# A two-layer block on one core: decay chain moved behind the gated products, one sigmoid moved ahead of two copies, and three transposes moved inside matmul units

## The reference

```python
u_lat = _modulate(h_lat, sh_m, sc_m)
q, k, v, g, glu, gates = _split_proj(u_lat @ p['w_in'] + p['b_in'])
lg_f = log_sigmoid(p['ret_decay_fwd']); lg_b = log_sigmoid(p['ret_decay_bwd'])   # 8 heads each
s_f = _retention_final_state(k_c, v_c, lg_f)          # context keys weighted by exp(distance * lg)
o, _, _ = _retention_bidir(q, k, v, lg_f, lg_b, s_f, s_b)
ret = silu(g) * _head_norm(o)
y_a = ret @ p['w_ret_out']
za, zb = split(glu); z = za * sigmoid(zb)             # the gated product
z = silu(_layernorm(_depthwise_conv(z, 31 taps)))
y_b = z @ p['w_conv_out'] + p['b_conv_out']
ga, gb = split(sigmoid(gates))
mix = (ga * y_a + gb * y_b) @ p['w_mix_out'] + p['b_mix_out']
```

## Time and profile before

| | |
|---|---|
| median of 3 runs | 1573.7 us |
| profiled execution | 1574.86 us, span 1573.0 us |
| TensorE busy | 1489.7 us, 95% of the span |
| VectorE, ScalarE, GpSimd busy | 708.4, 577.0, 411.3 us |
| mean granted TensorE clock | 0.988 of full speed |
| the stretch that the change touches | about 57 to 130 us, and 399 to 515 us |

### The profile page before, as it was taken

The page is one execution under the profiler, slowest core; times in us unless marked ns, Lnnn a source line. Parts: engine busy times, 40 slices in busy tenths (PEclk is TensorE's granted clock), DMA queues, the critical chain, the costliest instruction groups (busy, mean ns, idle before and its releaser), DMA issues.

```text
span 1573.0 us, 22932 instructions
## 1 busy us (share of the span) xinstructions
PE 1489.7 (95%) x9454; PEld 1033.6 (66%) x9454; DVE 708.4 (45%) x1292; ACT 577.0 (37%) x781; POOL 411.3 (26%) x314
## 2 busy tenths in 40 slices
PE   5999999999999899999999999889999899999998
PEld 3788888888666644444344344368888678878786
DVE  2578887575544841121111111244422644343674
ACT  2442425454343312222122112334344355465553
POOL 0000000010000100000000000149887686757564
PEclk9999999999999899999999999989999999999999
DMA  9722224436688789999999999747556353444432
GB/s 321 243 89 99 81 81 154 134 107 218 240 303 311 290 349 426 427 428 428 429 427 429 428 429 427 310 139 230 171 181 210 122 180 112 134 134 134 134 107 94
DMA packets 107330, 381.18 MB, mean 242 GB/s; under 512 B 7782, under 2 KB 9614, under 8 KB 94958
## 3 DMA queue, kind: packets, MB, share of 16 engines
q1 hardware_dynamic: 107246, 380.02, 63.9%
HBM read 378.95 MB, written 1.05 MB: 242 GB/s over the span
## 4 chain that ended last, share of the span: by engine, by line
PE 70%; DMA 15%; DVE 4%; ACT 4%; issue 1%; POOL 1%; SPq 0%; ACTq 0%; DVEq 0%; POOLq 0%
DMA arena<-in_w_exp_up 14%; PE ps L797 12%; PE ps L798 12%; PE ps L806 11%; PE ps L1222 9%; PE ps L1232 3%; PE ps L990 3%; PE ps L989 3%; PE ps L996 3%; PE ps L880 2%; ACT w_hi L2538 1%; PE ps L1243 1%; PE ps L1389 1%; POOL w_lo L2457 1%; DMA ring<-in_w_ret_out 1%
## 5 line engine op out<-in xcount | busy, mean ns | idle before, releaser
L2457 POOL TENSOR_TENSOR w_lo<-ring,w_hi 128x512 fp32r<-128x512 f32 x280 | 375.1, 1380 | 128.0 <-ACT w_hi L2538 116.3
L2538 ACT ACTIVATE w_hi<-ring 128x2048 fp32r<-128x2048 f32 x130 | 246.5, 1911 | 294.6 <-PE ps L806 130.8
L797 PE MATMUL ps<-w_hi,xt_hi 128*128 128x512 f32 x512 | 202.0, 394 | 0.0
L798 PE MATMUL ps<-w_hi,xt_lo 128*128 128x512 f32 x480 | 187.0, 390 | 0.0
L1526 DVE TENSOR_TENSOR w_lo<-ring,w_hi 128x2048 fp32r<-128x2048 f32 x60 | 138.0, 2303 | 93.1 <-ACT w_hi L2538 92.8
L1222 PE MATMUL ps<-arena 128*32 128x512 f32 x1408 | 155.4, 593 | 10.0 <-DMA arena<-in_w_exp_up 9.0
L797 PE MATMUL ps<-w_hi,yt_hi 128*128 128x512 f32 x352 | 139.6, 397 | 5.5 <-ACT w_hi L2538 3.0
L2457 POOL TENSOR_TENSOR w_lo<-ring,w_hi_ahead 128x512 fp32r<-128x512 f32 x8 | 9.9, 1275 | 480.3 <-ACT w_hi_ahead L2862 477.6
L806 PE MATMUL ps<-w_lo,xt_hi 128*128 128x512 f32 x512 | 126.7, 390 | 1.8 <-POOL w_lo L2457 1.8
L1222 PEld LDWEIGHTS ps<-arena 128*32 128x32 f32 x1408 | 49.7, 110 | 113.4 <-issue 112.1
L2120 DVE TENSOR_SCALAR selT<-ps 128x256 fp32r<-128x256 f32 x32 | 13.6, 424 | 237.8 <-ACT arena L2874 237.8
(11 more groups left out here) (328 smaller groups left out, 2361.3 us busy)
## 6 DMA issues: line engine op xcount, KB each, us to landing
arena<-in_w_exp_gate SPq DMA_DIRECT2D x22, 2048.0 KB, 29.9
arena<-in_w_exp_up SPq DMA_DIRECT2D x22, 2048.0 KB, 34.3
arena<-in_w_exp_down SPq DMA_DIRECT2D x21, 2048.0 KB, 33.5
ring<-in_w_in SPq DMA_DIRECT2D x40, 1024.0 KB, 5.1
ring<-in_b_w_in SPq DMA_DIRECT2D x40, 1024.0 KB, 5.1
ring<-in_a_w_in SPq DMA_DIRECT2D x24, 1024.0 KB, 5.1
ring<-in_w_exp_down SPq DMA_DIRECT2D x11, 2048.0 KB, 32.5
ring<-in_w_exp_gate SPq DMA_DIRECT2D x10, 2048.0 KB, 29.9
```

The costliest lines, as they stand in the source:

```text
L797: pe.matmul(o[:, tt, :], hi[:, k, x_], w[:, c, :], start=(bias is None and j == 0 and c == 0), stop=False)
L798: pe.matmul(o[:, tt, :], lo[:, k, x_], w[:, c, :], start=False, stop=False)
L2457: ins = pool.tensor_tensor(w_lo2[:, slots_of[n], k, :], ring[:, slots_of[n], k, :], w[:, k, :].bitcast(F32), ALU.subtract)
L2538: act.activation(part_of(n)[1][:, :, :], ring[:, slots_of[n]], ACT.Copy).then_inc(S("w_hi_full"), 1)
```

## The change

Five edits, all in the order of the lists; two of them also move work between places of one list:

1. VectorE: everything that computes the decays goes from ahead of `modulate(1, 0)` to later places. The two small operations stand behind `lo_of("glu", 3, 1)`, the chain and its four products behind `lo_of("k", 0, 1)`. `lo_of("glu", 2, 1)` now follows `lo_of("glu", 1, 1)` directly. Behind the chain come 12 taps in place of 20, then the scale of `wdec` with its wait for ScalarE's second Exp, then `lo_of("k", 1, 0)`. The 8 taps are left to later calls of `conv_taps`, which ends at the same total.
2. ScalarE: the first Exp goes behind `sigmoid_z(1)`, the second behind `turned_z(1)`.
3. ScalarE: `sigmoid_gate(3)` goes ahead of `lead_ret(2)` and `lead_ret(3)`.
4. TensorE: `turn_conv(0)` goes inside `ret_unit(1, 3)`, `turn_conv(1)` inside `conv_unit(0, 0)`, `turn_merged(1)` inside `mix_unit(0, 0)`, each as its `between`. The waits for the transposed halves move into `conv_unit`.
5. ScalarE and VectorE follow: `spread(3)` between the two conv halves, `gate_ret(1)` between their rests, `merge(1)` ahead of `lo_of("mix", 0, 0)`, `lead("mix", 1, 0)` ahead of `lead_part("mT", 1, ...)`.

```diff
@@ TensorE
+            def conv_unit(t, j, between=None):
+                if t == 0:
+                    pair_evacuated(pe, ("cvT", j))
+                gemm_unit("conv", t, j, xt2_hi, cv_lo, bias=BIAS_ROWS["conv"] + t, between=between)
             def turn_conv(c):
+                pe.wait_ge(S("cz_ready"), 1)
...
-            ret_unit(1, 3)
+            ret_unit(1, 3, between=lambda: turn_conv(0))
             spread_tail(3)
-            pe.wait_ge(S("cz_ready"), 1)
-            turn_conv(0)
-            turn_conv(1)
-            pair_evacuated(pe, ("cvT", 0))
-            conv_unit(0, 0)
+            conv_unit(0, 0, between=lambda: turn_conv(1))
             tail_unit(4, 0)
-            pair_evacuated(pe, ("cvT", 1))
...
-            mix_unit(0, 0)
-            turn_merged(1)
+            mix_unit(0, 0, between=lambda: turn_merged(1))
@@ VectorE (the moved chain and definitions are unchanged)
             lo_of("glu", 1, 1)
+            lo_of("glu", 2, 1)
+            modulate(1, 0)
+            u_rest(1, 0)
+            gated(0)
+            lo_of("glu", 3, 0)
+            modulate(1, 1)
+            u_rest(1, 1)
+            lo_of("glu", 3, 1)
             dve.wait_ge(S("load_decays"), 48)
...
-            lo_of("glu", 2, 1)
+            conv_taps(6)
+            lo_of("k", 0, 0)
+            gated(1)
+            lo_of("k", 0, 1)
             dve.wait_ge(S("decay_exped"), 1)
...
+            conv_taps(12)
             dve.wait_ge(S("decay_exped"), 2)
             dve.tensor_scalar(wdec, wdec, DK ** -0.5, None, ALU.mult).then_inc(S("wdec_ready"), 1)
-            conv_taps(20)
             lo_of("k", 1, 0)
...
-            for c in range(2):
-                rest_part("cvT", c, xt2_hi, cv_lo)
+            rest_part("cvT", 0, xt2_hi, cv_lo)
             gate_ret(1)
+            rest_part("cvT", 1, xt2_hi, cv_lo)
...
+            merge(1)
             lo_of("mix", 0, 0)
-            merge(1)
@@ ScalarE
             lead("glu", 2, 1)
-            (wait decay_asked 1, Exp of la)
             sigmoid_z(0)
...
             turned_z(0)
-            (wait decay_asked 2, Exp of wdec)
...
             sigmoid_z(1)
+            (wait decay_asked 1, Exp of la)
...
             turned_z(1)
+            (wait decay_asked 2, Exp of wdec)
...
             lead("ret", 0, 0)
+            sigmoid_gate(3)
             lead_ret(2)
             lead_ret(3)
-            sigmoid_gate(3)
...
             lead("conv", 0, 0)
+            lead_part("cvT", 0, xt2_hi)
             spread(3)
-            for c in range(2):
-                lead_part("cvT", c, xt2_hi)
+            lead_part("cvT", 1, xt2_hi)
...
             product_rows("tail", 5, 9)
+            lead("mix", 1, 0)
             lead_part("mT", 1, ot_hi)
             spread(5)
-            lead("mix", 1, 0)
```

More of the change, by code:

```diff
@@ L1087, in _, with ret_unit, mix_unit @@
             turn_ret(3)
-            def ret_unit(t, j):
+            def ret_unit(t, j, between=None):
                 if t == 0:
                     pair_evacuated(pe, ("retT", j))
[L1092 to L1097, removed]
+                gemm_unit("ret", t, j, yt_hi, rt_lo, nk=4, at=KC, between=between)
+            def conv_unit(t, j, between=None):
+                if t == 0:
+                    pair_evacuated(pe, ("cvT", j))
+                gemm_unit("conv", t, j, xt2_hi, cv_lo, bias=BIAS_ROWS["conv"] + t, between=between)
+            def mix_unit(t, j, between=None):
                 pair_evacuated(pe, ("mT", j))
-                gemm_unit("mix", t, j, ot_hi, ot_lo, bias=BIAS_ROWS["mix"] + t)
+                gemm_unit("mix", t, j, ot_hi, ot_lo, bias=BIAS_ROWS["mix"] + t, between=between)
             def tail_unit(t, j):
@@ L1591, in _ @@
             lo_of("glu", 1, 1)
[L1592 to L1595, removed]
             lo_of("glu", 2, 1)
[L1597 to L1626, removed]
             modulate(1, 0)
@@ L1683, in _ @@
             lo_of("glu", 3, 1)
-            dve.wait_ge(S("decay_exped"), 2)
-            dve.tensor_scalar(wdec, wdec, DK ** -0.5, None, ALU.mult).then_inc(S("wdec_ready"), 1)
+            dve.wait_ge(S("load_decays"), 48)
+            link(dve.tensor_scalar(la[:, 0, :], lg, -1.0, None, ALU.mult))
+            settle()
+            dve.tensor_tensor(la[:, 0, :], la[:, 0, :], lg, ALU.min).then_inc(S("decay_asked"), 1)
             conv_taps(6)
@@ L1689, in _ @@
             lo_of("k", 0, 1)
-            conv_taps(20)
+            dve.wait_ge(S("decay_exped"), 1)
+            link(dve.tensor_scalar(la[:, 1, :], la[:, 0, :], 2.0, None, ALU.add))
+            settle()
+            link(dve.reciprocal(la[:, 1, :], la[:, 1, :]))
+            settle()
+            link(dve.tensor_tensor(la[:, 0, :], la[:, 0, :], la[:, 1, :], ALU.mult))
+            settle()
+            link(dve.tensor_tensor(la[:, 1, :], la[:, 0, :], la[:, 0, :], ALU.mult))
+            settle()
+            link(dve.tensor_scalar(la[:, 2, :], la[:, 1, :], 2.0 / 17, 2.0 / 15, ALU.mult, ALU.add))
+            settle()
+            for n in (13, 11, 9, 7, 5, 3, 1):
+                link(dve.tensor_tensor(la[:, 2, :], la[:, 2, :], la[:, 1, :], ALU.mult))
+                settle()
+                link(dve.tensor_scalar(la[:, 2, :], la[:, 2, :], 2.0 / n, None, ALU.add))
+                settle()
+            link(dve.tensor_tensor(la[:, 2, :], la[:, 2, :], la[:, 0, :], ALU.mult))
+            link(dve.tensor_scalar(lg, lg, 0.0, None, ALU.min))
+            settle()
+            link(dve.tensor_tensor(lg, lg, la[:, 2, :], ALU.subtract))
+            settle()
+            dve.wait_ge(S("load_decays"), 48)
+            for d in range(2):
+                for tt in range(NT):
+                    ins = dve.tensor_scalar(wdec[:, d, tt, :], lg[:, H * d:H * (d + 1)], pos[:, d, tt:tt + 1], None, ALU.mult)
+                    if d == 1 and tt == 1:
+                        ins.then_inc(S("decay_asked"), 1)
+                    else:
+                        link(ins)
+            conv_taps(12)
+            dve.wait_ge(S("decay_exped"), 2)
+            dve.tensor_scalar(wdec, wdec, DK ** -0.5, None, ALU.mult).then_inc(S("wdec_ready"), 1)
             lo_of("k", 1, 0)
@@ L2634, in _ @@
             lead("glu", 2, 1)
-            act.wait_ge(S("decay_asked"), 1)
-            act.activation(la[:, 0, :], la[:, 0, :], ACT.Exp).then_inc(S("decay_exped"), 1)
             sigmoid_z(0)
@@ L2641, in _ @@
             turned_z(0)
-            act.wait_ge(S("decay_asked"), 2)
-            act.activation(wdec, wdec, ACT.Exp).then_inc(S("decay_exped"), 1)
             evacuate_x(3)
@@ L2649, in _ @@
             sigmoid_z(1)
+            act.wait_ge(S("decay_asked"), 1)
+            act.activation(la[:, 0, :], la[:, 0, :], ACT.Exp).then_inc(S("decay_exped"), 1)
             lead("k", 1, 0)
@@ L2653, in _ @@
             turned_z(1)
+            act.wait_ge(S("decay_asked"), 2)
+            act.activation(wdec, wdec, ACT.Exp).then_inc(S("decay_exped"), 1)
             lead("v", 0, 0)
```

## The result

The changed kernel takes 1563.1 us (median of six runs, 1558.1 to 1571.6) against 1572.9 us (median of six, 1570.7 to 1574.6). The ratio is 0.9946 with a 95% interval of 0.9928 to 0.9964. In a second series it was 1563.0 us, ratio 0.9949 (0.9921 to 0.9978). The profiled execution took 1563.49 us, its span 1561.6 us: 11.4 us under the profiled execution of before. The medians differ by 9.8 and 9.7 us. The intervals of the ratios (5.7 to 11.3 us and 3.5 to 12.4 us) hardly tell these from the 11.5 us of the forecast; what is missing was found in the profiles, term by term.

The account below looks back on a forecast made before the run. The prediction took TensorE, busy for 95% of the span, as the bound, leaving only its stops and half clock to regain. Terms 2.4 + 3.8 + 1.5 + 3.6 + 0.2 = 11.5 us gave 1562.2 us from 1573.7, range 1560.2 to 1567.0.

Parts of the forecast that it names:

- Part A, the stop: Ahead of `turn_z(0)`: stop shrinks from 2.70 to 0.67 us; with half clock and glu (3, 1)'s 0.48 us, 3.9 us gained.
- Part A, the new wait: At k (1, 0): TensorE waits 1.5 us for VectorE's remainder behind the second Exp; bounds nothing to 3.1 us.
- Part A, what else is queued: VectorE's later remainders lag 7 to 8 us at v (0, 0), with 4.8 us of cover left; counted as nothing.
- Part B: Ahead of ret (0, 0): sigmoid before the copies removes the stop, 2.2 us, and half clock, 1.6 us; 3.8 us.
- Part C: Ahead of conv (0, 0): moving the conv transposes removes the 1.5 us wait and none replaces it; 1.5 us.
- Part D: Ahead of mix (1, 0): an earlier leading part removes the stop, 2.0 us, and half clock, 1.6 us; 3.6 us.
- The half clock: Behind the stops of 2.70, 2.16 and 2.02 us TensorE runs at 1.2 GHz; 1.4, 1.6 and 1.6 us regained.
- Transposes as a pause: Rival, 4%: the 0.67 us stop plus 16 transposes count as one pause, 1.4 us is not regained; 1563.6 us.
- A new fall of the clock: Rival, 17%: half clock follows the 1.5 us stop at k (1, 0) or a like one; 1563.8 to 1565.4 us.
- Unit loads taking it back: Rival, 9%: full DMA engines set the pace, so the ret (0, 0) gain and half of mix's are lost; 1567.9 us.
- VectorE as the bound: Rival, 4%: from k (1, 0) on, ten remainders up to q (0, 1) each come 1.5 us late; 1577.2 us.
- The edit not doing what it says: Rival, 4%: another semaphore holds ret (0, 0) and mix (1, 0), so their stops stay; 1569.6 us.

Follow-up runs that it names:

- before_again: The kernel before the change, no edit, profiled a second time: 1572.6 us, span 1570.8 us.
- only_a: The kernel before with only VectorE's and ScalarE's order around the decays changed: 1569.4 us, ratio 0.9977 (ten runs).
- only_b: The kernel before with only `sigmoid_gate(3)` moved ahead of `lead_ret(2)` and `lead_ret(3)`: 1567.7 us, ratio 0.9964 (ten runs).
- only_c: The kernel before with only the conv transposes moved inside ret (1, 3) and conv (0, 0), copies and rests split accordingly: 1569.6 us, ratio 0.9987 (ten runs).
- only_d: The kernel before with only the mix edits (transposes, merge, leading part of mix (1, 0)): 1570.0 us, ratio 0.9983 (ten runs).
- fill_b: The kernel before with 20 unused identity transposes where TensorE stood still 2.16 us ahead of ret (0, 0): 1569.9 us (one run).
- after_again: The changed kernel once more, no edit, beside the kernel before: 1563.0 us (12 runs), ratio 0.9949.

## Why the prediction came out right, and where it didn't

The median was forecast at 1562.2 us and measured at 1563.1; the profiled execution at 1563.4 and measured at 1563.49. The near hit of the second is partly luck in how terms compensate:

- **Part A, the stop.** Forecast 2.70 to 0.67 us, measured 0.70 (0.70 in every profile that has the change). The 0.48 us stop went. Right. Its size of 0.48, though, belongs to the half clock ahead of it, as the point on the half clock shows.
- **Part A, the new wait.** Forecast 1.5 us, measured 1.35 to 1.39 in four profiles, released by w_lo, VectorE idle for 10.6 us ahead. Right. Its bound above, half clock behind it, never came.
- **Part A, what else is queued.** A step that failed: "all of VectorE's later remainders" was worked out for v (0, 0) and found covered, which holds, but the rope also frees a bank pair, and TensorE's context tile of k 1 needs that. 0.46 us more. The list of who waits for a delayed engine has to hold its releases of buffers, and not only its products. A gave 1.92 us for 2.4.
- **Part B.** Forecast 3.8 us, measured 3.67 up to ret (0, 3), where the stop grew from 0.98 to 1.28 us.
- **Part C.** Forecast 1.5 us, 1.8 in the changed kernel and 0.8 alone. The wait went, as forecast; how much of it is kept hangs on when conv (0, 0)'s and ret (1, 3)'s units land, and alone the part kept nothing up to the first expert.
- **Part D.** Forecast 3.6 us, measured 4.3 up to the first expert. The forecast cause holds in every part: the unit had landed, and only ScalarE's order kept it. The 0.2 us added for pipeline fills can't be told apart at these landmarks.
- **The half clock.** The term that was mis-sized, and in two ways. The sum took 4.6 us for it (1.4 + 1.6 + 1.6), as the one profile showed it at all three places. First, it does not always come: over the profiles that have the stop in question, half clock followed the 2.70 us stop 4 times of 6, the 2.16 us stop 2 of 5, the 2.02 us stop 4 of 6:

| profile | 2.70 us (A) | 2.16 us (B) | 2.02 us (D) | glu (0, 1) to gate 3's transposes | glu (0, 1) to first expert |
|---|---|---|---|---|---|
| before | half | half | half | 342.7 | 501.6 |
| before_again | half | full | half | 342.0 | 499.0 |
| only_a | - | full | half | 340.8 | 498.3 |
| only_b | full | - | full | 341.8 | 494.3 |
| only_c | half | full | half | 342.2 | 499.1 |
| only_d | half | half | - | 342.6 | 497.5 |
| fill_b | full | filled, full | full | 341.8 | 496.7 |
| after, after_again | - | - | - | 340.8, 340.8 | 489.9, 490.4 |

Second, at part A it costs less than 1.4 us where it comes. The fifth column shows it: 342.0 to 342.7 us with half clock behind the 2.70 us stop, 341.8 with full clock, 0.2 to 0.9 us between them and 0.6 in the mean. The sum overlooked a wait further on. With full clock TensorE gets through the transposes sooner and then stands longer for glu (3, 1)'s leading part. Here is TensorE's row in `only_b`, where the earlier trace rows have 0.48 us:

```profile
87.48 0.50 PE L797 MATMUL ps<-w_hi,yt_hi 128*128 128x512 f32 x1 [1.09 <-ACT w_hi L2538]
```

At B and D no wait behind takes it back: 1.7 and 1.8 us between profiles with and without, near the 1.6 of the sum. An estimate from these counts and prices is 4/6 of 0.6, 2/5 of 1.7 and 4/6 of 1.8: 2.3 us in place of 4.6. 11.5 - 2.3 = 9.2 us, beside medians of 9.8 and 9.7. That fits, but the counts are small and the intervals of the medians wide. The profile of before happened to be an execution with all three, 1574.86 us beside a median of 1572.9, and I took it down to the median by a flat 1.2 us instead of asking which terms of it were this execution's own.

- **The rivals.** Transposes as a pause: the 0.70 us stop with 16 transposes behind it was followed by full clock in all six profiles that have it, the 16 transposes and 1.4 to 1.5 us of stop ahead of conv (0, 0) in all eight, and the filled stops point the same way. The Trainium skill ("TensorE: Matmul & The Clock Gate", Part 4) says that a transpose doesn't count as busy for the clock gate in the same way as other work; these runs speak against it for the fp32 transposes of this kernel. A new fall of the clock: none at the new stop or at the old ones of 1.5 us, in any profile; even the 1.75 us ahead of ret (1, 3) in `only_c` had none. Unit loads taking it back: at most 0.3 us at ret (0, 3), and `only_d`, without part B, has the same 1.31 us there. VectorE as the bound: it came to v (0, 0)'s remainder at 134.1, with its product not waited for (the lag put at 7 to 8 us is 8.3 by the prediction's own numbers, still under its 11.6). The edit not doing what it says: no.

What is left is the spread of the changed kernel's runs, 1558 to 1574 us over 18 runs, with the kernel before at 1567 to 1585. The mean granted clock of each run goes with its time: the five shortest (up to 1560.4 us) have 0.993 to 0.996, the five longest (from 1570.5 us) 0.986 to 0.989. Span times (1 - clock) is the time that the lower clock took away; as an estimate from these figures it goes from 6.2 to 22.0 us, which is as wide as the spread of the runs. So most of the spread is half clock that comes in some executions and not in others. Not all of it, as two runs at 0.989 lie 5.6 us apart (1564.9 and 1570.5). In the profiles half clock also stands behind stops that no edit touched, in the router ahead of the experts and behind the experts' stage, and the first 57 us vary too (56.5 to 58.3). Where the long executions have theirs stays open, as none of them was profiled.

## What to carry to other kernels

Read a stop of TensorE as two prices, the stop itself and what may follow it at the lower clock, and put only a share of the second in the sum, taken from several profiles. Price it between two landmarks further apart, since a wait behind it can hide part of it (0.6 us for 1.4 at part A). When a chain of small operations is moved out of a critical place, look where its wait lands in the new list, and put the wait behind everything that doesn't need it: that was worth another 2.4 us here by the profiles. A copy whose data is there and that stands behind one whose data isn't (here a leading part behind a copy of transposes that were not made yet) is worth swapping; here it gave the 2.3 us of part D's stop.

## What the runs showed of the hardware that was not expected

- Behind the same stop of 2.0 to 2.7 us in the same place, TensorE's granted clock was 0.5 for about 3.4 us in 10 of 17 cases and 1.00 in the other 7, in the same program too (before and before_again at 2.16 us).
- TensorE filled with fp32 transposes through such a stop kept 1.00 in six of six cases (two profiles of one kernel). 16 transposes with a stop of 1.40 to 1.47 us behind them, 3.4 us together, were followed by 1.00 in eight of eight profiles.
- Over 18 runs of the changed kernel the granted clock went from 0.996 in the shortest to 0.986 in the longest, by the estimate above most of the 16 us between them.
- With 58 transposes added ahead of the loop over the experts three stops of about 5 us stood in that loop in both profiles, which nothing in the profile accounts for; with 20 added there were none (447.6 us for the stage).
